# Light experts multiplied unsplit in float32 by two 64-column operands, in units of 1792 columns, with down pieces used a unit later

## The reference

```python
logits = x @ w_router
top_vals, top_idx = lax.top_k(logits, 2)
gates = softmax(top_vals)
combine = einsum(one_hot(top_idx, 8), gates)
for e in range(8):
    out += combine[..., e] * ((silu(x @ we_gate[e]) * (x @ we_up[e])) @ we_down[e])
```

## Time and profile before

| | |
|---|---|
| median of 3 runs | 1277.2 us (1276.9 to 1277.87) |
| profiled execution, first to last instruction | 1276.0 us |
| profiled execution's time with what lies around the span | not recorded apart; the median is 1.2 us over the span |
| PE busy | 1227.3 us, 96% |
| DVE busy | 1106.1 us, 87% |
| ACT busy | 933.7 us, 73% |
| POOL busy | 39.8 us, 3% |
| read from DRAM, written | 428.40 MB, 4.98 MB |
| mean granted clock of TensorE | 0.994 |

### The profile page before, as it was taken

How to read it: one execution, slowest core, us unless ns; L and a number is a source line. 1 busy time by engine, 2 the same in 40 slices (tenths; PEclk the granted TensorE clock), 3 DMA queues, 4 the chain that set the end, 5 groups by cost and what they waited for, 6 DMA issues and landing times.

```text
span 1276.0 us, 15815 instructions
## 1 busy us (share of the span) xinstructions
PE 1227.3 (96%) x6181; PEld 1053.5 (83%) x6181; DVE 1106.1 (87%) x861; ACT 933.7 (73%) x716; POOL 39.8 (3%) x57
## 2 busy tenths in 40 slices
PE   9999999999999999999999999999999999999886
PEld 8988888888989888888887877888787888887664
DVE  6978555568889999999999999999999899999887
ACT  5575444445868787888888888887988888788774
POOL 0100000001010000000000000000000000000100
PEclk9999999999999999999999999999999999999998
DMA  9947555537459999999999999999999999999993
GB/s 317 346 163 262 190 182 192 198 110 254 159 171 348 370 410 399 398 412 411 409 409 401 411 409 412 411 394 408 411 410 410 412 405 408 411 411 404 412 411 159
DMA packets 143556, 434.49 MB, mean 341 GB/s; under 512 B 8964, under 2 KB 50996, under 8 KB 131188
## 3 DMA queue, kind: packets, MB, share of 16 engines
q1 hardware_dynamic: 139936, 421.07, 85.8%
q0 software_dynamic: 3456, 12.32, 2.8%
q10 hardware_dynamic: 84, 0.02, 0.0%
HBM read 428.40 MB, written 4.98 MB: 340 GB/s over the span
## 4 chain that ended last, share of the span: by engine, by line
PE 61%; DVE 17%; DMA 15%; ACT 5%; issue 2%; SPq 0%; ACTq 0%; DVEq 0%
DVE w_lo L1032 14%; DMA raw<-in_we_down 8%; PE turn L1686 7%; PE turn L1688 7%; PE turn L1687 7%; PE accp L1686 5%; PE accp L1687 5%; PE accp L1688 5%; DMA raw<-in_we_gate 5%; PE turn L1798 4%; PE turn L1795 4%; ACT w_hi L669 4%; PE turn L1797 2%; PE turn L1796 2%; DMA raw<-in_we_up 2%
## 5 line engine op out<-in xcount | busy, mean ns | idle before, releaser
L1032 DVE TENSOR_TENSOR w_lo<-raw,w_hi 128x1792 fp32r<-128x1792 f32 (+3 forms) x447 | 895.8, 2039 | 96.8 <-ACT w_hi L669 91.5
L669 ACT CAST w_hi<-raw 128x1792 fp32r<-128x1792 f32 (+2 forms) x441 | 756.0, 1724 | 173.9 <-PE turn L1688 43.2
L2130 PE MATMUL turn<-w_hi,t_both 128*128 128x448 f32 x512 | 193.8, 379 | 16.0 <-DVE w_lo L1032 15.4
L2131 PE MATMUL turn<-w_lo,t_both 128*128 128x448 f32 x512 | 188.7, 369 | 0.0
L1686 PE MATMUL turn<-w_hi,a_hi 128*128 128x448 f32 x496 | 184.0, 371 | 0.0
L1688 PE MATMUL turn<-w_hi,a_lo 128*128 128x448 f32 x496 | 181.7, 366 | 0.0
L1687 PE MATMUL turn<-w_lo,a_hi 128*128 128x448 f32 x496 | 181.7, 366 | 0.0
L2130 PEld LDWEIGHTS turn<-w_hi,t_both 128*128 128x128 f32 x512 | 97.5, 190 | 36.6 <-issue 20.0
L2131 PEld LDWEIGHTS turn<-w_lo,t_both 128*128 128x128 f32 x512 | 97.4, 190 | 7.9 <-issue 0.2
L1686 PEld LDWEIGHTS turn<-w_hi,a_hi 128*128 128x128 f32 x496 | 93.1, 188 | 9.8
L1687 PEld LDWEIGHTS turn<-w_lo,a_hi 128*128 128x128 f32 x496 | 93.2, 188 | 8.4
(11 more groups left out here) (298 smaller groups left out, 1529.8 us busy)
## 6 DMA issues: line engine op xcount, KB each, us to landing
raw<-in_we_gate SPq DMA_DIRECT2D x128, 896.0 KB, 8.6
raw<-in_we_up SPq DMA_DIRECT2D x128, 896.0 KB, 9.2
raw<-in_we_down SPq DMA_DIRECT2D x96, 1024.0 KB, 9.6
raw<-in_w_in SPq DMA_DIRECT2D x18, 1024.0 KB, 9.0
raw<-in_we_down SPq DMA_DIRECT2D x32, 512.0 KB, 8.6
raw<-in_w_down SPq DMA_DIRECT2D x11, 1024.0 KB, 5.1
raw<-in_w_gate SPq DMA_DIRECT2D x10, 1024.0 KB, 5.3
raw<-in_w_up SPq DMA_DIRECT2D x10, 1024.0 KB, 5.4
```

What stands on the lines that cost most here:

```text
L669: nc.scalar.copy(w_hi[:, p % PARTS, 0:filled(p)], raw[:, p % RING, 0:filled(p)]).then_inc(hi_done, 1)
L1032: return nc.vector.tensor_tensor(out, whole, hi.bitcast(f32), ALU.subtract)
L2130: nc.tensor.matmul(to[:, c, :], few, wh[:, kk, c, :], start=(k == 0), stop=False)
L2131: last = nc.tensor.matmul(to[:, c, :], few, wl[:, kk, c, :], start=False, stop=(k == KD - 1))
```

## The change

Light experts are no longer split. Their tokens stay in float32 (`x_few`, 64 columns), and PE multiplies weights straight from `raw` in float32. Each light unit takes 1792 columns: half of an expert, so that there are 8 light units and 16 heavy ones. A gate or up piece of it is one block of 128 input rows by 1792 columns. Its first 896 columns go to the sums in partitions 0 to 63 and its other 896 to partitions 64 to 127, each by a product with the same 64-column operand. So the sums fill all 128 partitions, silu, product and turn are those of a heavy unit, and the turned h (`hT_few`, one copy by ACT) holds 14 blocks of 64 columns. In down, the two halves of the output columns go to partitions 0 to 63 and 64 to 127 of one bank (`few_sum`). A light piece's raw slot comes free when PE has used it, and split buffers are counted over split pieces only (`part_of`). `add_low`, `fold_ys`, `few_low`, `raise_low` and the packed operands go.

The order of units becomes HHH, LHH six times, LHL. Down pieces are taken up to two units after their own: a light unit takes the 8 down pieces of the two heavy units before it, a heavy unit 4 of the 8 down pieces of a light one (8 in unit 22). Unit 1 has none, and the last unit's 8 follow at the end. Heavy h has two pairs of buffers (`hT_parts`). PE waits for `ys_kept` before the first down product of an expert. The additions of gathered rows (`add_rows`) move to behind the last unit, and the last expert's sums leave by one copy by ACT and are scattered in float32, by 64 partitions for each half of the columns.

```diff
-    ORDER = "HHH" + "LH" * 12 + "H" + "L" * QUARTERS
+    ORDER = "HHH" + "LHH" * 6 + "LHL"
+    UNITS_OF = {"H": 4, "L": 2}
+    ROWS_PIECES = {"H": 4, "L": 8}
...
-    VISITS = ((2, 0), (3, 1), (8, 2), (10, 3), (13, 4), (16, 5), (20, 6))
-    SUM_AT = (1, 4, 5, 6)
+    VISITS = ((2, 0), (4, 1), (8, 2), (10, 3), (13, 4), (16, 5), (20, 6))
+    SUM_AT = (1, 3, 5, 6)
...
+    def downs_in(i):
+        if i < 2:
+            return []
+        if i == 2:
+            return [(0, pair) for pair in range(4)]
+        if light(i):
+            return [(of, pair) for of in (i - 2, i - 1) if not light(of) for pair in range(4)]
+        if light(i - 1):
+            return [(i - 1, pair) for pair in range(4 if not light(i + 1) else 8)]
+        return [(i - 2, pair) for pair in range(4, 8)]
...
     def mixed(i):
-        return "uuuu" if i == 0 else "uuuudddd" if i == N_UNITS - 1 else "uduududd" if light(i) else "uduuuddd"
+        if not downs_in(i):
+            return "uuuu"
+        if not light(i):
+            return "ududuudd" if len(downs_in(i)) == 4 else "uduududddddd"
+        return "udududuuduuu" if len(downs_in(i)) == 4 else "ududududuudduudd"
...
-    WHOLE = {PLACE[piece] for piece in (("down", N_UNITS - 3, 1), ("down", N_UNITS - 2, 2))}
+    WHOLE = {PLACE[piece] for piece in PLACE if light(piece[1])}
...
+                if light(i):
+                    load(PLACE[which, i, pair],
+                         expert_rows(w, ORDER[i], k)[:, pair:pair + 1, 2 * s * WIDE:2 * (s + 1) * WIDE])
...
-                    pool.wait_ge(piece_used, upto((gate_piece, up_piece)[j - TOP_K](N_UNITS - 2, 1)))
+                    pool.wait_ge(piece_used, upto(last_down(units("H", 2)[-1])))
...
-                    nc.scalar.copy(ys_rows[0:FEW, :], few_sum[FEW:P, :]).then_inc(few_y_low, 1)
+                    nc.scalar.copy(ys_rows[:, 0:BANK], few_sum).then_inc(ys_kept, 1)
...
+            def keep_last():
+                used(MOE_AT + MOE_PIECES - 1)
+                act.wait_ge(acc_added, added(ALL_ROWS))
+                nc.scalar.copy(last_rows_in, few_sum).then_inc(last_kept, 1)
...
-            def add_low(i, which):
-                to = (few_gate, few_up)[which]
-                pe.wait_ge(few_kept, 2 * number(i) - 1 + which)
-                for c in range(2):
-                    last = nc.tensor.matmul(to[:, c, :], raise_low[:], few_low[:, c * PART:(c + 1) * PART],
-                                            start=False, stop=True, skip_group_check=True)
...
+            def few_down(i, pair):
+                _, s = expert_step(i)
+                half, quarter = divmod(pair, 4)
+                w = unsplit(down_piece(i, pair)).rearrange("p (j d) -> p j d", d=D)
+                hT = hT_few[:].rearrange("p (b h t) -> p b h t", h=2, t=FEW)
+                for j, block in enumerate(blocks_of(quarter)):
+                    for rows, cols in zip(HALVES, LAST):
+                        last = nc.tensor.matmul(few_sum[rows, :], hT[:, block, half, :], w[:, j, cols],
+                                                start=(s == 0 and pair == 0 and block == 0),
+                                                stop=(s == 1 and pair == 7 and block == BLOCKS - 1))
+                last.then_inc(piece_used, 1)
+            def few_rows(i, which, k):
+                e, _ = expert_step(i)
+                to = (gate_banks, up_banks)[which]
+                w = unsplit((up_piece if which else gate_piece)(i, k)).rearrange("p (h c f) -> p h c f", h=2, c=2)
+                for c in range(2):
+                    for h, rows in enumerate(HALVES):
+                        last = nc.tensor.matmul(to[rows, c, :], x_few[:, e % 2, k, :], w[:, h, c, :],
+                                                start=(k == 0), stop=(k == KD - 1))
+                last.then_inc(piece_used, 1)
...
             def down(i, pair):
-                _, s = expert_step(i)
+                kind, (e, s) = ORDER[i], expert_step(i)
                 if pair == 0:
-                    pe.wait_ge(e_hT_lo, i + 1)
...
+                    turned_left(i)
+                    if s == 0 and e:
+                        pe.wait_ge(ys_kept, KEPT.index((kind, e - 1)) + 1)
...
                 for n in range(NT):
...
+                    for rows, cols in zip(HALVES, LAST):
+                        nc.tensor.matmul(last_bank(n, cols), pickT[rows, 1, n * P:(n + 1) * P].bitcast(f32),
+                                         last_rows_in[rows, :], start=True, stop=True).then_inc(scattered, 1)
```

More of the change, by code:

```diff
@@ L154, in filled @@
         which, _, pair = IN_ORDER[p - MOE_AT]
-        return len(blocks_of(pair)) * D if which == "down" else 2 * WIDE
+        return len(blocks_of(pair % 4)) * D if which == "down" else 2 * WIDE
     ctx = ExitStack()
@@ L439, in last_bank, with rows_written @@
             return turn[:, 2 * n + (cols.start == BANK), :cols.stop - cols.start]
-        def last_sum(cols):
-            half, at = divmod(cols.start, BANK)
-            return accp[:, 2 + half, at:at + cols.stop - cols.start]
+        def rows_written(j):
+            return 16 * sum(2 if kind == "L" else 1 for kind, _ in KEPT[:j])
         token_rows_in = [ys_rows[:], more_rows[:]]
@@ L910, in _ @@
             for i in range(N_UNITS):
[L911 to L912 removed]
+                b = last_gate(i) + 1
+                ahead = last_up(i) + 3
+                if i and kept_at(i - 1) is not None and light(i):
+                    keep_ys(kept_at(i - 1))
                 if i:
                     round_h(i - 1)
[L915 to L918 removed]
@@ L919, in _ @@
-                if kept_at(i) is not None:
-                    keep_ys(kept_at(i))
-                if not light(i):
-                    leave_gate(i)
+                splits(b, b + 2)
+                leave_gate(i)
                 if i in (1, 2):
                     scale_tokens(i - 1)
-                unit_end = gate_piece(i, 0) + (U_PIECES if i else U_PIECES - 4) - 1
+                turned = up_piece(i, 2) + 3 if light(i) else min(b + len(mixed(i)) - 1, ahead)
+                splits(b + 3, turned)
@@ L926, in _ @@
+                leave_turned(i)
+                if light(i) and kept_at(i) is not None:
+                    kind, k = KEPT[kept_at(i)]
+                    before = last_down(units(kind, k)[-1]) + 4
+                    splits(turned + 1, before)
+                    keep_ys(kept_at(i))
+                    turned = before
                 if i == N_UNITS - 1:
                     break
-                silu_at = b + 4 if light(i) else b + 3
-                splits(b + 3, silu_at)
-                if light(i):
-                    silu_few(i)
@@ L2202, in turned_left @@
             def turned_left(i):
-                pe.wait_ge(e_hT_lo, i + 1)
+                pe.wait_ge(few_hT if light(i) else e_hT_lo, number(i))
             def writes_amid_up(i):
@@ L2283, in _ @@
                     before_gate(i)
-                    for pair in range(4):
+                    for pair in range(ROWS_PIECES[ORDER[i]]):
                         if pair == 1:
```

340 lines of the change are left out of this document (113 added, 227 removed).

## The result

The changed kernel takes **1314.97 us** (median of 4 runs, 1313.77 to 1318.81) against 1277.05 us for the kernel before in the same series (1276.55 to 1277.87). The ratio is 1.0302, with a 95% interval of 1.0287 to 1.0317. The forecast was 1265 us with a range up to 1289, so both the sign and the range were wrong. The profiled execution took 1315.47 us, its span 1313.7.

The account below looks back on a forecast made before the run. The prediction took DMA, bytes over rate, to bound the expert stage. Its terms gave 1276.0 - 10.4 + 2 - 4 = 1263.6 us of span, plus 1.2 makes 1264.8, say 1265 us; range 1256 to 1289.

Parts of the forecast that it names:

- PE's work: Expert stage: 1.50 us for a light piece with both halves side by side, PE 777 us in all, under DMA.
- Rival A: Light pieces on PE: halves run one after the other, 3.01 us a piece, 1457 us; chance 0.17 full, 0.05 partial.
- Changes of shape: PE switching between 64-column and full-width products: taken as free; 29 us if some 180 changes cost 0.16 us each.
- PE's new slack of about 70: PE's spare time under DMA over the changed expert stage, about 70 us, room for 29 us of shape changes.
- Removed work at no gain: Light pieces' casts on ACT and rests on DVE, 190 of each, go; they ran beside DMA, so no time gained.
- Transfers, -10.4 us: Light gate and up pieces travel in packets of 7168 bytes, at 421 GB/s in place of 406: 10.4 us gained.
- Ring and order, +2 us (0 to +8): Light raw slots come free only after PE's use; three pieces in flight suffice, a brief DMA stop costs 2 us.
- the weak place: First light unit: all four split buffers full, six raw slots hold light pieces, DMA stops briefly, 2 us.
- The end, -4 us: From the last weight landing to the span's end: 18.5 us in place of 22.5, gaining 4 us.
- B: Light units: halves overlap, but starvation and a halved clock eat the gain; 1276 to 1293 us, chance 0.12.

## Why the prediction was wrong, step by step

**PE's work: right.** The open question, whether two products on different halves of the array run beside each other, went as taken: 1.505 us for a light piece against 1.50. Rival A, which lives from 3.01 us, is out. The Trainium skill, TensorE: Matmul & The Clock Gate, Part 3, says that products on different tiles of the array run concurrently, and the trace agrees for two halves in float32: twice the speed of one after the other.

**Changes of shape: put too low.** They were put at nothing. In the pair from 708.14 to 712.78 the light up occupies 1.66 us until the next start, not 1.50, and the down 2.98, not 12 x 0.228 = 2.74: 0.40 us for a pair, two changes. The sum had allowed 29 us for them "inside PE's new slack of about 70". That slack was an average over the stage, and where the changes occur there is none: 4.24 us of products against 4.67 of transfers leave 0.43, and the changes take 0.40 of it. With eight slots the same changes stand at 413 GB/s, so by themselves they lower no rate; what part they have in the loss at six was not measured. The drain that the Trainium skill, TensorEngine Tiling (Array Packing), Key Properties, names fits these delays of 0.16 to 0.24 us; what else might cause them was not tested.

**Removed work at no gain: right.** 389 us of DVE and 349 of ACT went, and the time did not follow.

**Transfers, -10.4 us: right in size.** 9.8 measured, with the 128 further transfers of that run in it, so the packets alone may be worth less. The Trainium skill, DMA: Bandwidth & Descriptors, Why small descriptors are slow, gives a cost for each packet from which an estimate of 3.8 us follows. The measurement is 2.6 times that, and here the row of the trace was the better guide to what this edit of the transfers brings.

**Ring and order, +2 us (0 to +8): the step that failed.** The last landing came at 1295.4 in place of 1243.3, the one with eight slots: this term was 52 us (50.6 by the medians of the two kernels). The sentence that failed is "three stay in flight. That is thinner than now but enough". No row stood behind "enough". Two rows that were there spoke against it. Pieces took 8.6 to 9.6 us to land, nearly four transfers long, at full rate, so three in flight are fewer than the kernel had at its full rate; the run with five slots, at some three in flight, later put 26 us on that. And the slot of a light up was reckoned from the down ahead of it in steady state, "PE reaches a down 4.3 us after it lands", without following that 4.3 us onto PE at the first such border, where PE has run up to the landing edge and has to stand still for them. The prediction looked for "the weak place" at the first light unit only, where split buffers are full. It is at the opposite place, in each of the light units, where they are empty.

A second reading in this term failed too: that two light ups of 3 us would cover ACT's copy of finished down sums (`ys_kept`). PE waits for this copy three times, 2.06, 2.71 and 2.00 us, and behind the first two the granted clock falls (to 0.67 from 608 to 612 us and 0.58 from 836 to 840). In the case below ACT had first cast two heavy downs, the second when it landed, and began the copy at 833.69:

```profile
834.79 0.47 PE L1658 MATMUL accp<-w_hi,t_both 128*128 128x512 f32 x1 [2.71 <-ACT ys_rows L908]
```

With eight slots one such wait is left, 1.19 us. What these waits cost by themselves no run shows; they are part of the 52 us.

**The end, -4 us: right, in part by luck.** 18.3 us from the last landing to the end, 18.5 forecast. The order of things is the forecast one: ACT's copy waits for DVE's addition. But the scatter was reckoned at full clock, eight records one after the other, 3.4 us, with up to 3.5 more if the clock were halved. The clock is near half (0.54), and the scatter still takes 3.65 us: its products by 64 partitions run beside each other, two records in 0.86 us. The two errors cancel.

```profile
1297.88 1.28 DVE L1513 SCALAR_TENSOR_TENSOR x<-a_lo,small,x 128x1024 f32<-128x1024 f32 x1
1299.26 0.58 ACT L966 COPY more_rows<-accp 128x512 f32<-128x512 f32 x1 [20.02 <-DVE x L1513]
1299.99 3.65 PE L2103 MATMUL turn<-more_rows,pickT 64*128 64x512 f32 x8 [2.46 <-ACT more_rows L966]
```

```profile
1300.00:1302.00 2.00, 2.00 (x6) 1.11 (x8) 0.04 (x1) 0.00 (x0) 0.00 (x0) 0.54 0.03 8
```

**The rivals.** B had the mechanism (starvation and clock eat the gain, PE behind DMA at each heavy pair, slots waiting on PE) and the sign, at a chance of 0.12, with 2 us for a light unit. 52 us over eight light units is 6.5 each. The measured time is above its 1293. Its condition was wrong as well: in the gates PE is busy 2.76 and 3.15 of 4 us and the clock stays at 1.00 (684 to 692). It falls after the pause. Its own signs, "SP waiting for PE in pieces over 4 us, DMA share under 1 in the light units", are what the profile shows.

**What was put right and what is open.** With two raw slots in place of one split buffer from the first light gate on, the change gives 1264.4 us, and the forecast's other terms come out about as stated. Not tried: the same exchange in the kernel before (by its code ACT casts four pieces ahead of copies for which PE waits, so with three buffers each would wait for the other). Whether more slots alone would speed that kernel up is open. No run has more than six slots beside four split buffers, so what the split buffer that was given up costs in the expert stage is not shown either.

## What to carry to other kernels

When an edit moves the release of a load slot from an early consumer to a late one, follow one slot through the worst border of the order, from its landing to its release, and compare its longest hold with the ring; an average of busy time over the stage says nothing of it. A ring that is "always waiting" in the profile may be at its edge: one run with one slot fewer prices a slot, and it is an edit of one number. Work that is taken off a producer leaves its buffers too big, and that memory belongs to the resource that is now short, from the moment on when it is.

## What the runs showed of the hardware

- DMA's share stands at 1.01 to 1.03 both at 396 and at 431 GB/s (the window from 688 to 692 us of the changed kernel); a share of 1 does not show that the rate is full. Rate and landing time have to be read beside it.
- Between packets of 3584 and 7168 bytes the transfers still differ: 9.8 us on 117.4 MB, 3.4% of the 289 us that these bytes take at 406 GB/s, with 128 more transfers for the short packets.
- The sixth raw slot was worth 26 us in the kernel before and 63 us in the changed one, at the same number of bytes.
- A float32 product of 64 columns on one half of the array costs nothing in time beside one on the other half; changing between these and full-width products costs some 0.2 us each time (1.505 us for eight records; 0.16 and 0.24 us in the pair from 708.14).
